# TensorE waits for its own two broadcast products before it goes on with the projection: a 12-stage float32 transformer on one Trainium2 core

## What is computed

```python
def rms_norm(x, g):
    xf = x.astype(jnp.float32)
    y = xf * lax.rsqrt(jnp.mean(xf * xf, axis=-1, keepdims=True) + RMS_EPS)
    return (y * g.astype(jnp.float32)).astype(x.dtype)

def swiglu(x, w_gate, w_up, w_down):
    return (jax.nn.silu(x @ w_gate) * (x @ w_up)) @ w_down

    ...
    x = x + rms_norm(h, norm_mix_post[layer])
    h = rms_norm(x, norm_ffn_pre[layer])
    x = x + rms_norm(swiglu(h, ...), norm_ffn_post[layer])
```

## Time and profile before

| what | value |
|---|---|
| median of 3 runs | 2113.95 us (2107.89 to 2118.49) |
| profiled execution, its own time | 2115.64 us |
| span of the profile, first to last instruction | 2113.8 us |
| mean granted TensorE clock | 0.980 |
| TensorE busy (PE) | 96% of the span |
| VectorE / ScalarE / GpSimd busy | 66% / 45% / 2% |
| mean DMA rate | 162 GB/s |

### The profile page before, as it was taken

The page is one execution under the profiler, slowest core; times in us unless marked ns, Lnnn a source line. Parts: engine busy times, 40 slices in busy tenths (PEclk is TensorE's granted clock), DMA queues, the critical chain, the costliest instruction groups (busy, mean ns, idle before and its releaser), DMA issues.

```text
span 2113.8 us, 37138 instructions
## 1 busy us (share of the span) xinstructions
PE 2034.9 (96%) x15066; PEld 1892.9 (90%) x15066; DVE 1388.6 (66%) x1853; ACT 944.5 (45%) x1258; POOL 33.1 (2%) x48
## 2 busy tenths in 40 slices
PE   7999999999999999999998999999999996999998
PEld 7879989999979989998987888999899895799997
DVE  6767756666767756774667575776577457666773
ACT  4554434443554444444343454444444343644442
POOL 0000000000000000000000010000000000000000
PEclk9999999999999999999998889999999998999999
DMA  7335554444325554555530223455455543143553
GB/s 304 141 120 185 184 207 175 173 160 160 140 96 186 186 209 160 186 202 179 216 115 1 101 90 130 166 192 209 148 193 196 208 177 138 51 160 115 193 198 111
DMA packets 49789, 341.46 MB, mean 162 GB/s; under 512 B 5777, under 2 KB 6545, under 8 KB 9617
## 3 DMA queue, kind: packets, MB, share of 16 engines
q1 hardware_dynamic: 45216, 321.21, 42.2%
q10 hardware_dynamic: 4464, 18.68, 2.4%
HBM read 338.82 MB, written 1.05 MB: 161 GB/s over the span
## 4 chain that ended last, share of the span: by engine, by line
PE 86%; DVE 10%; ACT 2%; issue 1%; POOL 1%; DMA 0%; DVEq 0%; SPq 0%; POOLq 0%; ACTq 0%
PE pj L230 15%; PE pj L232 15%; PE pj L231 15%; PE acc L236 6%; PE acc L237 6%; PE acc L238 6%; PE pj L236 2%; PE pj L238 2%; PE pj L237 2%; PE pj L571 2%; DVE wlo L306 2%; PE pj L577 1%; PE acc L637 1%; PE acc L650 1%; PE mb L661 1%
## 5 line engine op out<-in xcount | busy, mean ns | idle before, releaser
L306 DVE TENSOR_TENSOR wlo<-raw,whi 128x2048 fp32r<-128x2048 f32 x285 | 653.0, 2291 | 301.0 <-ACT whi L299 300.0
L230 PE MATMUL pj<-xh,whi 128*128 128x256 f32 x2704 | 763.6, 282 | 13.6 <-DVE wlo L316 12.8
L231 PE MATMUL pj<-xl,whi 128*128 128x256 f32 x2704 | 759.9, 281 | 0.0
L232 PE MATMUL pj<-xh,wlo 128*128 128x256 f32 x2704 | 759.7, 281 | 0.0
L299 ACT ACTIVATE whi<-raw 128x2048 fp32r<-128x2048 f32 x299 | 569.8, 1910 | 419.6 <-PE acc L238 200.8
L230 PEld LDWEIGHTS pj<-xh,whi 128*128 128x128 f32 x2704 | 510.7, 189 | 16.7 <-issue 15.5
L231 PEld LDWEIGHTS pj<-xl,whi 128*128 128x128 f32 x2704 | 519.0, 192 | 0.1
L232 PEld LDWEIGHTS pj<-xh,wlo 128*128 128x128 f32 x2704 | 510.2, 189 | 0.0
L236 PE MATMUL acc<-whi,AR 128*128 128x512 f32 x656 | 257.0, 392 | 2.6 <-DVE AR L776 2.3
L237 PE MATMUL acc<-whi,AR 128*128 128x512 f32 x656 | 255.6, 390 | 0.0
L238 PE MATMUL acc<-wlo,AR 128*128 128x512 f32 x656 | 255.5, 390 | 0.0
(11 more groups left out here) (358 smaller groups left out, 2368.6 us busy)
## 6 DMA issues: line engine op xcount, KB each, us to landing
raw<-in_wstream SPq DMA_DIRECT2D x302, 1024.0 KB, 4.8
F<-in_gains ACTq DMA_DIRECT2D x12, 512.0 KB, 4.3
F<-in_rpb ACTq DMA_DIRECT2D x3, 1024.0 KB, 4.8
XM<-in_memtok ACTq DMA_DIRECT2D x2, 1024.0 KB, 4.7
XM<-in_memin ACTq DMA_DIRECT2D x2, 1024.0 KB, 6.8
F<-in_small ACTq DMA_DIRECT2D x1, 1536.0 KB, 10.6
F<-in_xin SPq DMA_DIRECT2D x2, 512.0 KB, 6.2
xt<-in_xtok SPq DMA_DIRECT2D x1, 1024.0 KB, 11.9
```

What stands on the lines that cost most here:

```text
L230: nc.tensor.matmul(o, wh, k_hi, start=first, stop=False, skip_group_check=True)
L231: nc.tensor.matmul(o, wh, k_lo, start=False, stop=False, skip_group_check=True)
L232: return nc.tensor.matmul(o, wl, k_hi, start=False, stop=last, skip_group_check=True)
L306: nc.vector.tensor_tensor(wlo[:, gs, :], raw[:, gs, :], whi[:, gs, :].bitcast(F32), ALU.subtract).then_inc(w_lo, 1)
```

## The change

After the two broadcast products `slices_pe` makes TensorE wait for the semaphore that the second of them raises. Nothing else is changed; no product, copy or transfer is added, taken away or moved.

```diff
--- before.py
+++ after.py
@@ -589,6 +589,7 @@
             w.g += n
             w.p += n
             bcast_pe(pe, tag, rsc[:, 2:4])
+            pe.wait_ge(*at(tag, "bc", 1))
 
 
         def score_bank(u, U, i):
```

## The result

| | before | after |
|---|---|---|
| median of 12 runs each, on one chip | 2114.61 us (2105.15 to 2119.9) | 2089.70 us (2084.07 to 2101.63) |
| ratio, 95% interval | | 0.9888 (0.9872 to 0.9904) |
| profiled execution, span | 2115.64 us, 2113.8 us | 2086.02 us, 2084.2 us |
| mean granted TensorE clock | 0.980 | 0.983 |

The changed kernel is 24.9 us faster, 20.3 to 27.1 us by the interval. The forecast was 3.5 us slower and a range that began at 2110.5 us. It was wrong in sign.

A forecast was written before the change was run, and what follows sets the result against it. TensorE, busy 96% of the span, was taken to bound the kernel. Each of eleven turns would lose 0.30 + 0.02 = 0.32 us, 3.5 us in all, taking 2113.95 us to 2117.5 us; range 2110.5 to 2124.5 us.

The forecast's parts named there:

- The wait: At eleven turns between stages, L230 starts 0.30 us later, 0.06 us after the products end; 0.32 us a turn with restart.
- The step behind it: L230 to L232 after the wait keep the same step, 0.11 to 0.12 us, so no gain or loss there.
- What the restart costs: First matmuls behind the products: the third is 0.34 us behind the first instead of 0.32, adding 0.02 us a turn.
- the bounds: Price of the wait at the eleven turns: 2.6 us in all from below, 5.0 us from above, never negative.
- The list of signs: What the changed profile should show: L230 0.66 us after L369 starts, ffn stages 0.3 us longer, mean clock 0.980 +- 0.005.
- The first (no cost): At the turns TensorE's queue would be held anyway, so the wait costs nothing; 2114 to 2116 us, chance 0.14.
- The third (clock at the turns): Clock also falls in dense chunks behind the wait, 3.4 us each; 13.7 us slower with three, 2127.7 us, chance 0.05.
- The second (clock in dsa): New idle time before dsa's 8-column matmuls doubles the low-clock loss, 3.4 us more; 6.9 us slower, 2120.9 us, chance 0.11.
- The fourth: Later work meets fewer low-clock stretches, which cost 42 us; over 0.5% faster needs 14 of them saved, chance 0.03.
- In the ffn stages TensorE has no idle time: In an ffn stage TensorE is busy 189.48 of 190 us, so it cannot catch up; all eleven delays count.
- The prediction's other sum, 2.9 us: Eleven waits with the skill page's 219 ns matmul latency, ending the products 0.056 us earlier; 2.9 us instead of 3.5.

The follow-up runs named there:

- the early products with a wait: Against the kernel before: both broadcast products moved ahead of the eighth slice, and TensorE waits for its last slice matmul before the third chunk; 2114.64 us, ratio 1.0013.
- the first fifteen kernels of the table: All kernels in the study's results table, original and changed ones included, except the last, which put the identity in place of the broadcast weights (2093.5 us, one run).

## Why the prediction was wrong

**The wait: right.** At each of eleven turns the next matmul (`L230` in nine, `L236` in two) starts 0.06 us behind the end of the products and, where it is `L230`, 0.66 to 0.67 us behind their start (0.66 forecast), the restart adds 0.02 us, VectorE's idle time before `L376` is the same 40.3 us in 11 times, and the first stage is untouched. The same price shows in the early products with a wait: 338 and 222 ns for two steps instead of 118 and 118, again 0.32 us. Eleven times 0.32 us, 3.5 us, stands.

**The step behind it: wrong, and this is what failed.** In *What the restart costs* stands: "After that the step is the same in both rows, 0.11 to 0.12 us: the drained pipeline does not run on more slowly, nor faster", and under the bounds "No reason in the rows makes this price negative". Rows of 0.01 us can't carry that sentence. The two levels, 113.3 and 117.8 ns, are both "0.11 to 0.12". Over 960 matmuls a difference of 0.0044 us is 4.3 us, thirteen times the 0.32 us of the wait that stands in front of them. The mean lengths of the groups, in whole ns, would have shown two levels in the kernel before as well: it ran its slices mostly at 113, and all ffn chunks at 118. The list of signs did name the right one, "if the step of L230 to L232 behind the wait were another than 0.12 us", but gave it no price and no chance. In the terms of the sum: the step behind the wait was put at nothing, and it measured 6 x 960 x 4.44 ns = 25.6 us of gain against the 3.5 us of cost. So an ffn stage is not 0.3 us longer, as forecast, but 3.9 us shorter (186.10 against 190.03 us).

**The rivals.** The first (no cost) is refuted by the timeline. The third (clock at the turns) did not come: the ffn stages are at 1.00, the whole at 0.983 (forecast 0.980 +- 0.005). The second (clock in dsa) named as its sign a longer stretch of low clock, and the profile of the changed kernel has one, beside the earlier trace rows:

```profile
1689.00:1695.00 6.00, 6.00 (x37) 0.63 0.83 308
1695.00:1700.00 5.00, 5.00 (x25) 0.50 0.79 315
1700.00:1706.00 6.00, 6.00 (x51) 0.94 0.00 0
```

By the sum of the prediction that is 10.2 us at the lower level instead of 6.8, and the part of the dsa stage up to the products of the memory is 1.8 us longer. But the changed kernel profiled again has 6.9 us there, as the kernel before:

```profile
1697.00:1703.00 6.00, 6.00 (x41) 0.72 0.81 296
1703.00:1708.00 5.00, 5.00 (x31) 0.65 0.81 301
```

So it moves between executions of one kernel, and these two profiles do not show that the wait lengthens it. The fourth had the right sign with the wrong mechanism; fewer stretches of low clock account for none of the gain, since the changed kernel gained as much (0.9865 to 0.9896) when it was profiled at 0.980.

**"In the ffn stages TensorE has no idle time"** was right too, and is why 4.4 ns of each matmul came through in full.

The Trainium skill ("TensorE: Matmul & The Clock Gate", section "Back-to-back issue gap") says that in a stream of weight loads and matmuls the spacing is set by both operations. The traces here agree that the two go together. In 96 stretches of 40 us, six in each kernel, the loads of `L230`, `L231` and `L232` are all recorded as 188 ns wherever the step is 113 (59 stretches), and exactly one of the three as 192 ns wherever it is 118 (37 stretches); mostly it is `L231`, with the early products and a wait `L230`. Which of the two sets the other is not shown. The prediction's other sum, 2.9 us, rested on a latency that the same page, section "Single matmul latency", gives for bf16; these products are float32, and `L230` started 57 ns behind their recorded end, so the record was the right basis.

**What stays open** is why there are two levels, and what in such weights turns them over, with two or four products but not with three. Nor is it shown why a break directly ahead of or behind the two products keeps the stream from ending at 118: in all 51 such places the level behind was 113, also in the two where the slices had come in at 118, so that there the pair and the break together rather lead to 113 than keep what was. Nothing of how the engine does it shows in a trace.

## What to carry to other kernels

Where an engine runs thousands of equal instructions back to back, compare the mean length or the distance between starts in ns over a long stretch, before and after; timeline rows of 0.01 us hide a 4% change of rate, and here that was worth seven times the wait under study. A few odd matmuls at the entrance to a long stream can set its rate: look at the level ahead of them and behind them, and if it changes, try them one at a time between other work, or with a break beside them. When a change makes busy time shrink at an equal count and an equal clock, no account of waits will explain it.

## What the runs showed of the hardware

- A stream of float32r matmuls with 128 x 128 weights and 256 columns, each with its own weight load, runs at 113.3 or 117.8 ns a matmul at a granted clock of 1.00, and keeps its level for hundreds of matmuls. At 118 one of three weight loads is recorded as 192 ns and the others as 188, at 113 all as 188.
- Two float32 products with one column repeated as weights, in an unbroken stream, took the level from 113 to 118 (50 of 50 places) and from 118 to 113 (11 of 13); four took it from 113 to 118 (9 of 9). Three kept it (113 eight times, 118 once), and so did two with the identity as weights (113 fourteen times, 118 once). One kept 113 (36 of 36) and twice was followed by 113 where the stream had been at 118. Four transposes took it from 118 to 113 (131 of 133).
- In the ffn stages the level was kept through a pause of 0.06 us in which TensorE waits for its own last matmul (118 five times, 113 once); over the longer breaks of 0.33 and 0.43 us between two chunks it was kept four times and changed twice. Started by VectorE at `L577`, the slices ran at 113 in most cases, and at 118 in 18 of the 165 turns of the first fifteen kernels of the table.
- TensorE starts 0.06 us after the end of its own matmul that it waits for, as it does after VectorE's.
